# Grouped heads of the first attention: scores by two rounded-format products instead of one full-precision product

## What the reference computes

```python
MLA_HEADS, MLA_QK = 8, 96          # "other heads": 96 numbers per query and key
GQA_HEADS, GQA_KV_HEADS, GQA_DIM = 8, 2, 64   # "grouped heads": 64 numbers, 4 heads share one key
Q_BLOCK = 128

def attend(q, k, v):
    ...
    def block(qi):
        s = jnp.einsum('bqgrd,bsgd->bgrqs', qi, k).astype(jnp.float32) * scale
        p = jax.nn.softmax(s, axis=-1).astype(v.dtype)
        return jnp.einsum('bgrqs,bsgd->bqgrd', p, v)

def even_mixer(h_lat, h_ctx, ...):
    ...
    ka, va = jnp.concatenate([ka_c, ka_l], axis=1), jnp.concatenate([va_c, va_l], axis=1)
    kb, vb = jnp.concatenate([kb_c, kb_l], axis=1), jnp.concatenate([vb_c, vb_l], axis=1)
    out_lat = merge(attend(mla_q(cq_l, ...), ka, va), attend(gqa_q(gq_l, ...), kb, vb))
    if need_ctx_out:
        out_ctx = merge(attend(mla_q(cq_c, ...), ka_c, va_c), attend(gqa_q(gq_c, ...), kb_c, vb_c))
```

## Time and profile before

| | us |
|---|---|
| median of 3 runs | 3826.52 |
| lowest and highest | 3816.03, 3827.30 |
| profiled execution | 3815.25 |
| its span in the trace | 3813.9 |
| TensorE busy | 3692.4 (97%) |
| VectorE busy | 2357.7 (62%) |
| ScalarE busy | 1523.0 (40%) |

### The profile page before, as it was taken

One profiled execution on the slowest core, in us unless ns is written; L12 is line 12 of the kernel. 1 busy time (PEld: TensorE's weight loads), 2 busy tenths in 40 slices (PEclk: granted clock), 3 DMA queues, 4 the chain that ended last, 5 costly groups with the idle time before them and its releaser, 6 DMA issues.

```text
span 3813.9 us, 50961 instructions
## 1 busy us (share of the span) xinstructions
PE 3692.4 (97%) x20580; PEld 3107.2 (81%) x20580; DVE 2357.7 (62%) x3602; ACT 1523.0 (40%) x2446; POOL 266.6 (7%) x209
## 2 busy tenths in 40 slices
PE   7999999999999998999999999999999999969999
PEld 4868778888888866788889986899977888748998
DVE  5446566765556346544488877888743344488886
ACT  3245443323234424323354445544432222475443
POOL 0000001860000010000000011000020000200000
PEclk8999999999999989999999999999999999999999
DMA  5200012333322201232233332233322232203332
GB/s 215 94 28 1 1 44 87 130 131 119 133 90 70 72 23 34 83 100 95 91 105 101 102 100 78 88 110 103 106 78 87 96 100 89 78 7 91 109 106 93
DMA packets 233145, 330.38 MB, mean 87 GB/s; under 512 B 14416, under 2 KB 151248, under 8 KB 232912
## 3 DMA queue, kind: packets, MB, share of 16 engines
q1 hardware_dynamic: 230320, 320.40, 26.1%
q10 hardware_dynamic: 2592, 6.74, 0.5%
HBM read 324.99 MB, written 2.10 MB: 86 GB/s over the span
## 4 chain that ended last, share of the span: by engine, by line
PE 84%; DVE 6%; ACT 2%; issue 1%; POOL 0%; ACTq 0%; DVEq 0%
PE ps L837 17%; PE ps L839 17%; PE ps L838 17%; PE ps L1749 5%; PE ps L1751 5%; PE ps L1750 5%; PE ps L2148 2%; PE ps L2133 1%; PE ps L2123 1%; PE ps L2124 1%; PE ps L2028 1%; PE ps L2029 1%; PE ps L2030 1%; PE ps L3241 1%; PE ps L3239 1%
## 5 line engine op out<-in xcount | busy, mean ns | idle before, releaser
L837 PE MATMUL ps<-t 128*128 128x512 f32 (+1 forms) x2608 | 953.1, 365 | 4.2 <-DVE t L3643 2.7
L838 PE MATMUL ps<-t 128*128 128x512 f32 (+1 forms) x2608 | 945.5, 363 | 0.0
L839 PE MATMUL ps<-t 128*128 128x512 f32 (+1 forms) x2608 | 944.5, 362 | 0.0
L436 DVE TENSOR_TENSOR t<-t 128x1024 fp32r<-128x1024 f32 (+2 forms) x454 | 538.1, 1187 | 292.9 <-ACT t L423 289.9
L423 ACT ACTIVATE t<-t 128x1024 fp32r<-128x1024 f32 (+2 forms) x454 | 458.0, 1010 | 627.0 <-PE ps L839 427.6
L837 PEld LDWEIGHTS ps<-t 128*128 128x128 f32 x2608 | 495.9, 190 | 87.4 <-issue 7.3
L838 PEld LDWEIGHTS ps<-t 128*128 128x128 f32 x2608 | 495.8, 190 | 77.3 <-issue 2.5
L839 PEld LDWEIGHTS ps<-t 128*128 128x128 f32 x2608 | 495.3, 190 | 76.9
L1749 PE MATMUL ps<-blocks_hi,t 128*128 128x256 f32 x1416 | 400.4, 283 | 13.9 <-ACT t L1778 11.0
L1751 PE MATMUL ps<-blocks_hi,t 128*128 128x256 f32 x1416 | 397.0, 280 | 0.0
L1750 PE MATMUL ps<-blocks_lo,t 128*128 128x256 f32 x1416 | 396.9, 280 | 0.0
(11 more groups left out here) (486 smaller groups left out, 5799.1 us busy)
## 6 DMA issues: line engine op xcount, KB each, us to landing
t<-w_up SPq DMA_DIRECT2D x88, 512.0 KB, 3.5
t<-w_ada SPq DMA_DIRECT2D x160, 256.0 KB, 3.2
t<-w_s_up SPq DMA_DIRECT2D x138, 256.0 KB, 3.6
raw_more<-w_s_up SPq DMA_DIRECT2D x126, 256.0 KB, 3.5
t<-w_s_up SPq DMA_DIRECT2D x44, 512.0 KB, 3.3
t<-w_down SPq DMA_DIRECT2D x32, 512.0 KB, 3.6
raw_more<-w_s_down SPq DMA_DIRECT2D x54, 256.0 KB, 2.7
t<-w_s_down SPq DMA_DIRECT2D x42, 256.0 KB, 2.6
```

The lines of the kernel that those rows point to most:

```text
L436: k.V.tensor_tensor(lo, self.slot(self.raw_at[n])[:, 0:self.size(n)], hi.bitcast(F32), ALU.subtract).then_inc(self.lo_done.sem, 1)
L837: k.T.matmul(out, wh, hh, start=(i == 0), stop=False)
L838: k.T.matmul(out, wh, hl, start=False, stop=False)
L839: ins = k.T.matmul(out, wl, hh, start=False, stop=(i == len(kts) - 1))
```

## The change

- `QL`, `QC` and `K` are placed at fixed addresses (from `HEADS`), no longer taken from the allocator.
- A tile `QG` (128 rows, `fp32r`) holds for each grouped head the rounded query in one half of the rows and its rest in the other; a pair `KP` holds the rounded keys and their rest in all 128 rows. `QG` lies over `K`, `KP` over `QL`.
- Each grouped score is the sum of two `fp32r` products with 128 rows: `QG` with `KP.hi`, then `QG` with `KP.lo`, accumulated in the same bank. A wide unit has four such products of 384 columns, a narrow one has two of 256.
- Ten splits (eight queries, two keys) make these tiles: a Copy on ScalarE, then a subtraction on VectorE, each over 768 columns. They are put into the instruction streams of steps 8, 14, 20, 26, 32, 38, 40, 42, 46 and 52: on ScalarE behind the exponential of that step, on VectorE between the scaled maximum of that step and the result of unit i-3. Each waits until the scores that read the overwritten tile are done.
- TensorE's grouped scores wait for the splits they need.
- The semaphores of `gqa_` and `unit_` are handed on after the stage.

```diff
-    def __init__(self, k, units, probs, turned, ready=(), values_ready=(), free=(), result=None):
+    def __init__(self, k, units, probs, turned, ready=(), values_ready=(), free=(), result=None, beside={}):
...
         k.pe.wait_ge(self.ex.at(i - 1))
-        if nk <= 512:
+        if "low" in u:
+            k.pe.wait_ge(u["split"])
+            parts = [(s, slice(0, nk))] if nk <= 512 else [(s, slice(0, nk // 2)), (s + 1, slice(nk // 2, nk))]
+            for b, keys in parts:
+                to = k.ps[:, b, 0:keys.stop - keys.start]
+                k.T.matmul(to, u["q"], u["k"][:, keys], start=True, stop=False)
+                ins = k.T.matmul(to, u["q"], u["low"][:, keys], start=False, stop=True)
+            ins.then_inc(self.sc.sem, 1)
+        elif nk <= 512:
...
                 self.act_exp(i)
+            if i in self.beside:
+                act_split, dve_split, x = self.beside[i]
+                act_split(x)
...
                 self.dve_max(i)
+            if i in self.beside:
+                act_split, dve_split, x = self.beside[i]
+                dve_split(x)
...
-            QL = k.alloc(scope, 8, NL)
-            QC = k.alloc(scope, 8, NC)
-            K = k.alloc(scope, 8, NT)
+            QL, QC, K = k.place("mla_ql", HEADS, 8, NL), k.place("mla_qc", HEADS + 16384, 8, NC), k.place("mla_k", HEADS + 24576, 8, NT)
...
+            KP = k.place_pair("gqa_k", HEADS, 2, NT)
+            QG = k.place("gqa_q", HEADS + 24576, 8, NT, dt=F32R)
+            gh, gl = (k.event("gqa_" + n) for n in ("hi", "lo"))
+            splits = [("q", h) for h in range(5)] + [("k", 0), ("k", 1)] + [("q", h) for h in range(5, 8)]
+
+            def split(what, x):
+
+                if what == "k":
+                    return KG[:, x, :], KP.hi[:, x, :], KP.lo[:, x, :], 36
+                a, b = (slice(0, 64), slice(64, 128)) if x % 2 == 0 else (slice(64, 128), slice(0, 64))
+                return GR[a, x // 2, :], QG[a, x, :], QG[b, x, :], 6 * x + 6
+
+            def act_split(n):
+                src, hi, lo, units_before = split(*splits[n])
+                k.act.wait_ge(attend.sc.at(units_before))
+                k.A.activation(hi, src, ACT.Copy).then_inc(gh.sem, 1)
+
+            def dve_split(n):
+                src, hi, lo, units_before = split(*splits[n])
+                k.dve.wait_ge(gh.at(n + 1))
+                k.V.tensor_tensor(lo, src, hi.bitcast(F32), ALU.subtract).then_inc(gl.sem, 1)
...
-                        units.append(dict(q=GR[rows, h // 2, tb * 128:(tb + 1) * 128], k=KG[rows, g, 0:nk], nk=nk,
+                        units.append(dict(q=QG[:, h, tb * 128:(tb + 1) * 128], k=KP.hi[:, g, 0:nk], low=KP.lo[:, g, 0:nk],
+                                          split=gl.at(max(7, splits.index(("q", h)) + 1)), nk=nk,
...
+                           beside={i: (act_split, dve_split, n) for n, i in enumerate((8, 14, 20, 26, 32, 38, 40, 42, 46, 52))})
...
-        for name in ("att_", "mla_", "latent_"):
+        for name in ("att_", "mla_", "latent_", "gqa_", "unit_"):
```

More of the change, by code:

```diff
@@ L70 @@
 TOP = 172000
+HEADS = 180192
 MORE = 94624
@@ L2074 @@
 class Units:
-    def __init__(self, k, units, probs, turned, ready=(), values_ready=(), free=(), result=None):
-        self.k, self.units, self.probs, self.turned = k, units, probs, turned
+    def __init__(self, k, units, probs, turned, ready=(), values_ready=(), free=(), result=None, beside={}):
+        self.k, self.units, self.probs, self.turned, self.beside = k, units, probs, turned, beside
         self.ready, self.values_ready, self.free, self.result = ready, values_ready, free, result
@@ L2776, in even_mixer @@
             for h in range(8):
-                rows, g = slice(64 * (h % 2), 64 * (h % 2) + 64), h // 4
+                g = h // 4
                 for si, nk in ((0, NT), (1, NC)):
@@ L2787, in even_mixer @@
                            ready=t_mla + t_gqa, values_ready=[t_vm, t_v], free=[c_free] + t_mla + t_gqa,
-                           result=lambda i, b, m: k.V.tensor_scalar(units[i]["dst"], b[:, 0:64], m[:, 3:4], None, ALU.mult))
+                           result=lambda i, b, m: k.V.tensor_scalar(units[i]["dst"], b[:, 0:64], m[:, 3:4], None, ALU.mult),
+                           beside={i: (act_split, dve_split, n) for n, i in enumerate((8, 14, 20, 26, 32, 38, 40, 42, 46, 52))})
             attend.pe_program()
@@ L2793, in even_mixer @@
             attend.end()
+            gh.past(10)
+            gl.past(10)
         with ExitStack() as scope:
```

## The result

| | before | changed |
|---|---|---|
| median, us (20 runs each) | 3822.69 | 3802.05 |
| lowest and highest, us | 3816.03, 3827.49 | 3794.82, 3822.37 |
| ratio, 95% interval | | 0.995 [0.994, 0.996] |
| profiled execution, us | 3815.25 | 3796.74 |
| attention, start of the first score to start of the last result, us | 264.5 | 250.1 |

The change made the kernel 20.6 us faster; 22.1 was forecast. The runs scatter more than before: 11 us between the lowest and the highest became 28. The two profiled executions are 18.5 us apart. Of these, the attention is 14.4 us and what follows it 5.8; the attention starts 1.7 us later. There is one profile of the kernel before, of the lowest of its 20 runs.

The account below looks back on a forecast made before the run. TensorE alone was taken to bound the attention. Grouped heads gain 36.5 us, the splits take 14.4, leaving 22.1: from 3826.5 to 3804 us; forecast case 3797 to 3812, full range 3783 to 3818.

Parts of the forecast that it names:

- The step it began from: Attention, both halves: bound by TensorE and nothing else; VectorE and ScalarE have room.
- The grouped part of the sum: Eight grouped heads: 4.6 us gained in each, 36.8, less 0.3 at the passage between head kinds: 36.5 us.
- Grouped scores: Grouped heads: rounded products take 0.17 us (384 columns) or 0.12 (256); a wide unit's scores 0.69 instead of 1.49.
- The change of rows: Grouped heads: the 0.29 us a unit for changing between 64 and 128 rows goes, 14 us over eight heads.
- The rival that it stays: Grouped heads: the 0.29 us a unit comes from alternating scores and transposes; gain 8 us, 3818; chance 0.06.
- Order of the other engines: Grouped heads: with VectorE and ScalarE handovers a head takes 12.5 us, where TensorE alone would need 12.3.
- The rival of one unit at a time: Grouped heads: each unit passes VectorE and ScalarE in turn, a head 14.6 us; gain 6, 3821; chance 0.09.
- The splits: Ten splits in the attention: VectorE's queue behind them makes TensorE wait, costing 14.4 us together.
- the six like step 14: Splits at steps 8, 14, 20, 26, 32, 38: TensorE loses 1.9 us each, 11.2 in all.
- the late ones: Splits at steps 42, 46 and 52: they cost 1.6, 0.7 and 0.9 us.
- What comes after: Behind the attention: no load is on its way during the stage, so all that follows moves forward as one piece.
- The rival of the clock: Grouped heads: short scores and many transposes lower TensorE's clock, up to 96 us over eight heads, 3900; chance 0.07.

Follow-up runs that it names:

- the kernel with the copy first: Changed kernel with ScalarE's split copy before the exponential of its step, not behind it: 3790.4 us, ratio 0.9917; again 3784.9, 0.9901.
- one product: The kernel with the copy first, each grouped score made of the first product alone, without the keys' rest: 3778.5 us, ratio 0.9881 to before.
- filled: Changed kernel with two idle TensorE products put into the standstill at steps 8 to 38: 3800.9 us, ratio 0.9944 to before.
- splits-only kernel: Changed kernel's ten splits kept, grouped scores made as before in plain floats with 64 rows: 3846.3 us, ratio 1.0060 to before.
- the copy is made twice and filled: Changed kernel with ScalarE's split copy made twice and three idle TensorE products in the standstill at steps 8 to 38: 3813.6 us, ratio 0.9971.
- the copy twice: Changed kernel with ScalarE's split copy made twice behind the exponential, nothing filled: 3838.0 us, ratio 1.0042 to before.

## Why the prediction was right

The step it began from, that TensorE alone sets the time of the attention, holds, and so does each mechanism of the sum. The grouped part of the sum can be read by itself in the kernel with the copy first, where the splits cost nothing: its attention is 264.5 - 232.0 = 32.5 us shorter than before, 34.2 with its longer start, and 36.5 was forecast.

- **Grouped scores**: 0.17 and 0.12 us a product, as taken.
- **The change of rows**: gone, and shown alone to be worth 13.7 us in the medians and 13.9 in the attention (14 forecast). The rival that it stays is out.
- **Order of the other engines**: 12.83 us a head against 12.5 forecast. The 0.2 us of a late unit came as the rule had them. Of the difference, 6 × 0.05 = 0.3 us is the first score product behind value products. I had taken this seam as free because rows 4 have none between a rounded and a plain product. But it is not a matter of format: rows 2 have it between 0.70 and 0.65, both plain and both 384 columns, and I had used both numbers without asking why they differ. Over eight heads the gain was forecast 2.4 us too large. Why the first product takes longer was not tested. The rival of one unit at a time is out: with one product a head still falls to 11.7.
- **The splits**: 14.4 forecast. Without a fall of the clock the changed kernel's attention is 245.5 us (filled), with the copy first 232.0: 13.4 us. In the splits-only kernel it is 12.4, of which the six like step 14 are 11.3 (11.2 forecast) and the late ones 1.1 (3.2 forecast), which is the part of this term that was too large. The wait of 1.5 us, its place and its cause came as written; the second wait, for the exponential, was 0.2 us in the record of the weight load, 0.4 forecast.
- **What comes after**: the attention ends sooner and the rest follows. From the last result to the end it is 3277.6 us before, 3271.8 and 3276.6 in the two profiles of the changed kernel, and 3274 to 3286 in the others: a scatter from 6 us less to 8 more, as large as the errors of the sum.

The attention without a fall is 264.5 - 245.5 = 19.0 us shorter than before, the forecast 22.1. The seam explains 2.4 of it. The filled kernel also had the longer start of the stage, 12.8 us against 11.2, which is 1.5 us; that varies from profile to profile. The splits' 1.0 us less goes the other way: 2.9 of the 3.1.

That the forecast time (3804) comes within 2 us of the measured one (3802.05) is luck in part. The three runs of before had a median of 3826.5, and over twenty it is 3822.7, lower by more than the gain was missed. The 11.3 us between profile and median that the forecast carried over are 5.3 in the changed kernel (3796.74 and 3802.05). And the medians' 20.6 us are more than the two profiles show in the attention (14.4 and 9.2); the rest lies within the scatter of what comes after and is not located. One step of the range does not add up as written: splits at 19.6 and products at their bound together leave 36.5 - 19.6 - 7.7 = 9 us of gain, not 15, which is what the products' bound alone leaves. The measured gain lies well inside either.

**What was missing** is a second price of the standstill. The rival of the clock had the right effect from the wrong cause, and so in the wrong place: it blamed a mix of short scores and many transposes. The grouped heads, which have that mix, held 1.00 in every profile but for a few us behind the unfilled last split where the copy is made twice and filled; the other heads, with their waits of up to 1.5 us, did not. A fall took 5.1 us in one profile, about 10 in the other (255.3 - 245.5). The sum has no term for it, and that the forecast held in spite of it is luck in part: both profiles have a fall behind one of six splits only, and its cost is no larger than the scatter. How often the other runs had one is not known.

The trace of the kernel before had the sign. TensorE waits 2.58 us before 277.24 and 2.23 us before 542.59, and the clock is low behind both (0.66 in the window below, 0.50 in rows 8), while gaps of up to 1.21 us in the stretch of the second block's attention in rows 8 left it at 1.00. The two standstills, and the window of the first:

```profile
277.24 1.44 PE L2123 MATMUL ps<-t 96*128 96x384 f32 x2 [2.58 <-ACT t L2177]
...
542.59 0.44 PE L2812 MATMUL ps<-t 128*128 128x128 f32 x2 [2.23 <-DVE t L2834]
...
277.00:282.00 5.00, 4.76 (x14) 3.05 (x15) 0.83 (x3) 1.65 (x5) 0.00 (x0) 0.66 0.00 0
```

## What to carry to other kernels

Work put "beside" other work is free only if no one queues behind it: before adding it, write down what stands behind it on each engine and until when that is needed. When two engines hand work to each other, start the first half in a wait that the engine has anyway (here ScalarE's wait for the maximum), and the whole of it costs nothing, as it did here (15.36 us a head with and without). A short standstill of TensorE should be priced at its length plus the risk of the low clock behind it, which, when it came in the changed kernel, cost 5.1 us behind 1.50 and about 10 behind 1.49; and where two equal products differ by 0.05 us in the chain of waits, ask why before carrying one of them over.

## What the runs showed of the hardware

- Standstills of 1.24 to 1.50 us, one in 17 us, brought the granted clock down behind one split and not behind the others of the same execution, and behind none in splits only; with standstills of 1.5 to 2.4 us it fell at all six. The fall to 1.2 GHz lasted some 10 and 20 us in the two profiles of the changed kernel although TensorE was busy again all that time (windows of 4.00 us busy at 0.50), and some 3 to 24 us with the copy twice.
- Idle products in the gap kept the clock at 1.00 at every filled split, in the one profile of each of the two kernels, and cost nothing where TensorE would have waited (heads of 17.2 us with and without).
- A change between products of 64 and of 128 rows costs 0.14 to 0.15 us. Between 96 and 128 rows it costs nothing: with all products on 128 rows they take as long as in the heads with 96 (0.70, 0.65, 0.22, 1.29 us).
- The first score product behind value products of 64 columns costs 0.05 us more than the following, in both formats (0.23 and 0.17; 0.70 and 0.65).
